# Experts of a mixture: whole low parts on GpSimd, the operand's split on ScalarE and VectorE, and matmuls with the high part ahead of the wait for the low part

## The chip, the core and the metric

The kernel runs on one core of one Trainium2 chip. The core has engines that run side by side and are ordered by semaphores alone: TensorE (matmuls, PE in the profile, with its weight loads as PEld), VectorE (DVE), ScalarE (ACT), GpSimd (POOL) and SyncE (SP), which here only issues DMAs. TensorE, VectorE, ScalarE and GpSimd read and write SBUF; matmul results go to PSUM, eight banks of 512 floats in each of 128 partitions. The metric is the time of the whole program on the device in microseconds, lower being better.

## What is computed

The reference is a two-layer backbone over 512 latent and 256 context tokens of width 1024, in float32. Each layer mixes tokens (four mixers, gates, a projection) and then runs an expert-choice mixture of 16 experts, which is the part that the change touches:

```python
def _expert_choice_ffn(h, w_router, w1, w3, w2):
    cap = CAPACITY_FACTOR * T // N_EXPERTS
    aff = jax.nn.softmax((h @ w_router).astype(jnp.float32), axis=-1)
    vals, idx = lax.top_k(aff.transpose(0, 2, 1), cap)
    xg = jax.vmap(lambda hb, ib: hb[ib])(h, idx)
    hid = jax.nn.silu(jnp.einsum('becd,edf->becf', xg, w1)) * jnp.einsum('becd,edf->becf', xg, w3)
    y = jnp.einsum('becf,efd->becd', hid, w2) * vals[..., None].astype(h.dtype)
    return jax.vmap(lambda yb, ib: jnp.zeros((T, D), h.dtype).at[ib.reshape(-1)].add(yb.reshape(-1, D)))(y, idx)
```

An expert takes 64 latent rows and, in the first layer only, 32 context rows. In the second layer the context is not carried on.

## The kernel before

Matmuls run on operands rounded to a shorter float format. To keep float32 accuracy each operand is split in two: a high part, which is the rounded value (a copy), and a low part, which is the value less the high part (a subtraction). Every product is then three matmuls: high with high, high with low, low with high.

The weights of an expert are three matrices of 1024 x 1024. They are cut in 12 blocks of 512 rows by 512 columns (128 partitions x 2048 floats, 1 MB): blocks 0, 1, 4, 5 of the gate matrix, 2, 3, 6, 7 of the up matrix, 8 to 11 of the down matrix (`expert_block`). Each block b goes through the same stations:

- SyncE issues its DMA into `raw`, a ring of four buffers (`RING`), once the split of the block four places earlier is done (line 594 and the two waits ahead of it).
- ScalarE writes the high part (`hi`, line 1522) into one of three pairs of buffers (`expert_part`, of which two lie in `part` and one in `hx`), once TensorE is done with the block three places earlier (`ring_used`). It counts `split_h`.
- VectorE writes the low part (`rest`, line 2077) and counts `split_v`. For the blocks 1, 3, 5, 7 (`G_HALVES`) it writes half of it, and GpSimd the other half (line 798), counting `split_g`.
- TensorE waits for the low part, all of it, and runs 12 matmuls of 512 columns (line 1253): for each of four slices k the three products.

The expert's rows, `xg_hi` and `xg_lo`, are the other operand of blocks 0 to 7. GpSimd copies and subtracts them (lines 781 and 785), once block 7 of the expert before is done, and TensorE waits for both (`xg`) ahead of an expert.

Each engine works through its own list in order; two experts, an even one (j = 0) and an odd one (j = 1), make one turn of a loop, eight turns a layer. ScalarE and VectorE split two blocks ahead (`AHEAD`): at place b they split block b + 2. Between the splits stand the other steps of an expert. On ScalarE: the Silu behind blocks 1 and 5, the high part of the hidden values (`hd_hi`, at 6 and 9), the high part of y (`y_hi`, line 1546, at 10 and 11, after `val`), and one table load at the start of a turn. On VectorE: the product into `hid` (at 3 and 7), the low part of the hidden values (at 6 and 9), `val` (line 2104, at 9), the matrix `put` that scatters the rows (line 2110, at 10), the low part of y (line 2125, at 10 and 11), and the adds of the scatter results (`add`, line 2085). On TensorE: behind block b of an even expert scatter b - 1 into bank 4, for which it waits for the add of the scatter before (`e_acc`); an odd expert has fewer of them and in the second layer none; the first scatter also waits for the low part of y (`e_yL`). Behind blocks 5 and 8 it transposes the hidden values, which wait for `hid`. On GpSimd: two DMAs (four in the first layer) that fetch `pair` for `val`, which wait until `put` is done (`e_put`), and only behind them the halves of the low parts.

## Time and profile before

| | us |
|---|---|
| median of three runs | 3880.74 (3878.51 to 3883.74) |
| the profiled execution | 3872.74 |
| its span, first to last instruction | 3870.8 |
| TensorE busy in the span | 3418.9 (88%) |
| VectorE busy | 2332.5 (60%) |
| ScalarE busy | 1624.7 (42%) |
| GpSimd busy | 1037.9 (27%) |

The expert stage of the first layer runs from about 1433 to 2130 us of the span, that of the second from about 3205 to 3820. Line 1253, the experts' matmuls, holds 774.6 + 372.7 us of TensorE's busy time. In the profile "busy" is the time from an instruction's start to its end, which includes time in which it is held up while running; a matmul's recorded length (0.39 us) overlaps the next one's, so what counts is the distance between starts. The number in square brackets behind an instruction is how long its engine stood idle before it, and what ended that.

### The profile page before, as it was taken

The page shows a single profiled execution, that of the slowest core. Times are in us where ns is not written, and L with a number is a line of the kernel's source. Part 1 is how long each engine was busy: PE and PEld are TensorE (multiplying, and loading weights), DVE is VectorE, ACT ScalarE, POOL GpSimd, SP SyncE. Part 2 cuts the span into 40 slices and gives each one's busy share as a digit, 9 for nine tenths or more (in the row PEclk, how much of TensorE's full clock was granted, in tenths as well). Part 3 has the DMA queues.
Part 4 walks back from the last instruction along what each step waited for, and adds up shares of the span by engine and source line. Part 5 has one row for each costly group of instructions (what it writes and reads, how often), then busy time and mean ns, then how long its engine had stood idle before and what let it go on. Part 6 is the DMA issues. An engine that isn't in the chain of part 4 may idle for free.

```text
span 3870.8 us, 49033 instructions
## 1 busy us (share of the span) xinstructions
PE 3418.9 (88%) x19072; PEld 2794.2 (72%) x19072; DVE 2332.5 (60%) x3395; ACT 1624.7 (42%) x2095; POOL 1037.9 (27%) x640
## 2 busy tenths in 40 slices
PE   6988899899999969998988199898999969999995
PEld 4988569888887847776776189678866657777774
DVE  2685751511111649989998765751422258999998
ACT  3213752511110236666665322653311126667763
POOL 2001012222120025555554100012222103434442
PEclk8989999999999979999999599998999979999998
DMA  7232034022222329888888122131132217999995
GB/s 241 98 131 94 24 97 143 12 71 67 75 87 77 120 92 313 309 300 307 311 312 318 49 83 78 49 99 55 39 98 98 81 73 265 335 328 342 338 334 205
DMA packets 331926, 633.91 MB, mean 164 GB/s; under 512 B 14526, under 2 KB 104910, under 8 KB 325358
## 3 DMA queue, kind: packets, MB, share of 16 engines
q1 hardware_dynamic: 309056, 557.88, 41.4%
q0 software_dynamic: 22704, 73.73, 5.8%
q8 instruction: 115, 1.88, 0.2%
q14 instruction: 51, 0.42, 0.0%
HBM read 615.05 MB, written 16.50 MB: 163 GB/s over the span
## 4 chain that ended last, share of the span: by engine, by line
PE 64%; DVE 16%; issue 8%; ACT 6%; DMA 3%; POOL 2%; POOLq 1%; DVEq 0%; ACTq 0%; SPq 0%
PE ps L852 42%; PE ps L1253 11%; DVE part L2077 3%; PE ps L977 2%; PE ps L1009 2%; POOL part L798 2%; DVE hx L2077 1%; PE ps L995 1%; ACT hx L1522 1%; DVE area L2085 1%; ACT area L1374 1%; DVE area L1681 1%; PE ps L997 1%; ACT part L1522 1%; DVE area L2104 1%
## 5 line engine op out<-in xcount | busy, mean ns | idle before, releaser
L852 PE MATMUL ps<-hx,part 128*128 128x384 f32 (+2 forms) x4704 | 935.2, 358 | 26.1 <-DVEq L532 22.0
L852 PEld LDWEIGHTS ps<-hx,part 128*128 128x128 f32 x4704 | 835.6, 190 | 114.7 <-DVEq L532 23.6
L1253 PE MATMUL ps<-part,hx 128*128 128x512 f32 x3072 | 774.6, 404 | 104.6 <-POOL part L798 70.9
L1253 PEld LDWEIGHTS ps<-part,hx 128*128 128x128 f32 x3072 | 582.1, 193 | 254.7 <-POOL part L798 85.2
L2077 DVE TENSOR_TENSOR part<-raw,part 128x2048 fp32r<-128x2048 f32 (+1 forms) x256 | 598.6, 2341 | 106.0 <-ACT part L1522 103.5
L1522 ACT ACTIVATE part<-raw 128x2048 fp32r<-128x2048 f32 x256 | 490.2, 1916 | 141.5 <-PE ps L1253 122.9
L518 POOL TENSOR_TENSOR part<-raw,part 128x2048 fp32r<-128x2048 f32 x52 | 238.2, 4580 | 858.7 <-ACT part L515 831.3
L1253 PE MATMUL ps<-hx 128*128 128x512 f32 x1536 | 372.7, 391 | 4.2 <-DVE hx L2077 3.8
L2077 DVE TENSOR_TENSOR hx<-raw,hx 128x2048 fp32r<-128x2048 f32 (+1 forms) x128 | 311.8, 2436 | 49.2 <-ACT hx L1522 48.8
L1253 PEld LDWEIGHTS ps<-hx 128*128 128x128 f32 x1536 | 287.4, 188 | 72.8 <-DVE hx L2077 5.5
L852 PE MATMUL ps<-part,hx 128*128 128x256 f32 (+2 forms) x2208 | 317.1, 306 | 17.7 <-DVEq L532 15.5
L852 PEld LDWEIGHTS ps<-part,hx 128*128 128x128 f32 x2208 | 296.7, 198 | 35.1 <-DVEq L532 16.1
L798 POOL TENSOR_TENSOR part<-raw,part 128x1024 fp32r<-128x1024 f32 x96 | 286.3, 2982 | 128.8 <-ACT part L1522 128.1
L1968 DVE TENSOR_TENSOR area<-ps,area 128x768 f32<-128x768 f32 (+1 forms) x48 | 39.6, 825 | 429.1 <-PE ps L852 429.1
L852 PE MATMUL ps<-area,raw 128*128 128x384 f32 (+1 forms) x768 | 285.3, 521 | 0.0
L1522 ACT ACTIVATE hx<-raw 128x2048 fp32r<-128x2048 f32 x128 | 244.7, 1912 | 25.9 <-PE ps L1253 20.1
L852 PEld LDWEIGHTS ps<-area,raw 128*128 128x128 f32 x768 | 145.0, 190 | 107.9 <-issue 46.0
L1681 DVE SCALAR_TENSOR_TENSOR area<-area,conv_c 128x512 f32<-128x512 f32 x360 | 208.5, 656 | 0.0
L515 ACT ACTIVATE part<-raw 128x2048 fp32r<-128x2048 f32 x76 | 144.8, 1906 | 127.5 <-DMA raw<-in_w_in 93.5
L1473 ACT ACTIVATE area<-ps,mgate_b 128x768 f32<-128x768 f32 x32 | 28.8, 901 | 349.8 <-PE ps L852 349.8
L852 PE MATMUL ps<-raw,area 128*128 128x256 f32 x640 | 144.3, 388 | 10.0 <-DMA raw<-in_w_out 10.0
L852 PEld LDWEIGHTS ps<-raw,area 128*128 128x128 f32 x640 | 124.1, 195 | 28.7 <-issue 11.4
(260 smaller groups left out, 3923.0 us busy)
## 6 DMA issues: line engine op xcount, KB each, us to landing
raw<-in_w_exp_gate SPq DMA_DIRECT2D x128, 1024.0 KB, 5.1
raw<-in_w_exp_up SPq DMA_DIRECT2D x128, 1024.0 KB, 5.4
raw<-in_w_exp_down SPq DMA_DIRECT2D x128, 1024.0 KB, 5.1
raw<-in_w_mod SPq DMA_DIRECT2D x48, 1024.0 KB, 7.7
raw<-in_w_in SPq DMA_DIRECT2D x44, 1024.0 KB, 5.2
raw<-in_w_gate SPq DMA_DIRECT2D x32, 1024.0 KB, 7.9
area<-in_bias POOLq DMA_DIRECT2D x32, 512.0 KB, 4.0
raw<-in_w_branch SPq DMA_DIRECT2D x16, 1024.0 KB, 7.2
```

What stands on the lines that cost most here:

```text
L515: nc.scalar.activation(part[:, q % 2, 0, :], raw[:, n % RING, :], ACT.Copy).then_inc(S("split_h"), 1)
L518: self.tt.tensor_tensor(part[:, q % 2, 1, :], raw[:, n % RING, :], part[:, q % 2, 0, :].bitcast(f32), ALU.subtract).then_inc(S("split_p"), 1)
L798: nc.gpsimd.tensor_tensor(expert_part(s, 1)[:, 2:4, :], raw[:, (r0 + s) % RING, :].rearrange("p (k n) -> p k n", k=4)[:, 2:4, :], expert_p ...
L852: last = mm(dst, a, b, start=i == 0, stop=i == len(pairs) - 1)
L977: last = mm(ps[h2 * HD:(h2 + 1) * HD, 6 + u % 2, 0:P], v, probT[:, w % NTURN, (2 * (b - b0) + h2) * P:(2 * (b - b0) + h2 + 1) * P], start= ...
L995: mm(ps[:, h2, 0:hi - lo], q, k[:, lo:hi], start=True, stop=True)
L1009: last = nc.tensor.transpose(ps[:, 4 + g % 2, o:o + P], prob[:, u % NPROB * 2 + h2, b * P:(b + 1) * P], ident)
L1253: last = mm(ps[:, bank, :], x, y, start=kh == 0 and a == 0, stop=kh == 1 and a == len(pairs) - 1)
L1522: fn(expert_part(s, 0), src, ACT.Copy).then_inc(S("split_h"), 1)
L1681: own(V.scalar_tensor_tensor(y, x, conv_c[:, j, tap:tap + 1], y, ALU.mult, ALU.add))
L1968: V.tensor_tensor(even(t_) if ctx_out else t_[:, 0:LAT], p_, s_, ALU.mult).then_inc(*S("z_part", l).by(1))
L2077: V.tensor_tensor(expert_part(s, 1)[:, ks, :], src[:, ks, :], expert_part(s, 0)[:, ks, :].bitcast(f32), ALU.subtract).then_inc(S("split_v" ...
```

## The change

What it does, by engine:

- The low parts of blocks 2 and 7 are written whole by GpSimd (`G_SPLITS`), those of the other ten whole by VectorE. `rest_rank` says whose a block is and how many of that engine's come before.
- The expert's rows are split by ScalarE (`operand_hi`, at place 8) and VectorE (`operand_lo`, at place 9, ahead of `val`), no longer by GpSimd. GpSimd's list of an expert is then the DMAs of `pair` behind `e_put` and two subtractions.
- TensorE waits at the start of a block for the high part only (`split_h`), runs the eight products with it (`x_hi` and `x_lo`), then waits for the low part and runs the four with that.
- SyncE's DMAs of the experts stand in a loop over eight turns, with computed addresses, instead of 192 instructions a layer. Each waits for one semaphore, that of the engine that wrote the low part four blocks earlier.

```diff
-G_HALVES = (1, 3, 5, 7)
+G_SPLITS = (2, 7)
-NG, NV = len(G_HALVES), EXP_BLOCKS
+NG, NV = len(G_SPLITS), EXP_BLOCKS - len(G_SPLITS)
...
+def rest_rank(s):
     e, b = s // EXP_BLOCKS, s % EXP_BLOCKS
-    return NG * e + sum(g < b for g in G_HALVES)
+    before = sum(g < b for g in G_SPLITS)
+    return (True, NG * e + before) if b in G_SPLITS else (False, NV * e + b - before)
...
+        def operand(e, j, full):
+            src = (xgT[:, :, e, :] if isinstance(e, int) else
+                   xgT[:, :, bass.ds(e, 1), :].rearrange("p k a c -> p k (a c)"))
+            return [(rows_of[j][0], src[:, :, 0:CAPL]), (high_of[j], src[:, :, CAPL:CAP]),
+                            (low_of[j], src[:, :, CAPL:CAP])][:3 if full == NT else 1]
...
-                for s in range(EXP_BLOCKS * E):
-                    name, c, kh = expert_block(s % EXP_BLOCKS)
-                    sp.wait_ge(S("split_v"), v0 + s + 1)
-                    if s >= RING and (s - RING) % EXP_BLOCKS in G_HALVES:
-                        sp.wait_ge(S("split_g"), g0 + halves_before(s - RING) + 1)
+                with sp.Fori(0, E // 2) as i:
+                    for j in range(2 * EXP_BLOCKS):
+                        gps, before = rest_rank(j - RING)
+                        if gps:
+                            sp.wait_ge(S("split_g"), i * 2 * NG + (g0 + before + 1))
+                        else:
+                            sp.wait_ge(S("split_v"), i * 2 * NV + (v0 + RING + before + 1))
+                        src = A[name][l, bass.ds(i * 2 + j // EXP_BLOCKS, 1), kh * NCH:(kh + 1) * NCH, c:c + NCH]
...
-                        pool.wait_ge(ring_used, i * 2 * EXP_BLOCKS + (B_EXP[l] + EXP_BLOCKS * j - 4))
-                        for at, x in moves:
-                            last = nc.gpsimd.tensor_copy(xg_hi[:, :, at], x)
-                        pool.drain()
-                        for at, x in moves:
-                            last = nc.gpsimd.tensor_tensor(xg_lo[:, :, at], x, xg_hi[:, :, at].bitcast(f32), ALU.subtract)
                         pool.wait_ge(*S("e_put", l).at(i * 2 + j + 1))
...
-                        for s in (EXP_BLOCKS * j + b for b in G_HALVES):
+                        for s in (EXP_BLOCKS * j + b for b in G_SPLITS):
                             pool.wait_ge(S("split_h"), i * 2 * EXP_BLOCKS + (h0 + s + 1))
-                            nc.gpsimd.tensor_tensor(expert_part(s, 1)[:, 2:4, :],
+                            nc.gpsimd.tensor_tensor(expert_part(s, 1),
...
-                        pe.wait_ge(*S("xg", l).at(i * 4 + 2 * j + 2))
+                        pe.wait_ge(*S("xg_lo", l).at(i * 2 + j + 1))
-                            pe.wait_ge(S("split_v"), i * 2 * NV + (v0 + RING + s + 1))
-                            if b in G_HALVES:
-                                pe.wait_ge(S("split_g"), i * 2 * NG + (g0 + halves_before(s) + 1))
+                            pe.wait_ge(S("split_h"), i * 2 * EXP_BLOCKS + (h0 + s + 1))
-                            pairs = [(x[:, 4 * kh + k, :], w[u][:, k, :]) for k in range(4)
-                                     for x, u in ((x_hi, 0), (x_hi, 1), (x_lo, 0))]
+                            pairs = [(x[:, 4 * kh + k, :], w[0][:, k, :]) for k in range(4) for x in (x_hi, x_lo)]
+                            pairs += [(x_hi[:, 4 * kh + k, :], w[1][:, k, :]) for k in range(4)]
                             for a, (x, y) in enumerate(pairs):
+                                if a == 8:
+                                    gps, before = rest_rank(s)
+                                    if gps:
+                                        pe.wait_ge(S("split_g"), i * 2 * NG + (g0 + before + 1))
+                                    else:
+                                        pe.wait_ge(S("split_v"), i * 2 * NV + (v0 + RING + before + 1))
...
                         if s + AHEAD < body or not final:
                             hi(i, s + AHEAD)
+                        if b == 8 and not (final and j):
+                            act.wait_ge(ring_used, i * body + (r0 + s))
+                            operand_hi(i * 2 + j + 1, 1 - j)
...
-                        if s + AHEAD < body or not final:
+                        if (s + AHEAD < body or not final) and not rest_rank(s + AHEAD)[0]:
                             rest(i, s + AHEAD)
                         for c in scatters(j, b, per):
                             add(c, 4, i * per)
+                        if b == 9 and not (final and j):
+                            operand_lo(i * 2 + j + 1, 1 - j, i * 2 + j + 2)
```

The diff's pieces are, in this order, of the constants, the helper for the operand, SyncE, GpSimd (twice), TensorE, ScalarE and VectorE.

Three places show what stands where in the engines' lists. Names in square brackets are the semaphores that an instruction waits for. TensorE, blocks 1 and 2 of an even expert, before:

```order
L1253 MATMUL ps<-part,hx 128x512 [waits split_g]
L1253 MATMUL ps<-part,hx 128x512 x11
L1258 ISA [waits e_yL]
L852 MATMUL ps<-hx 128x512 [waits e_acc]
L852 MATMUL ps<-hx 128x512
L1240 REGISTER_ALU
L1253 MATMUL ps<-hx 128x512 [waits split_v]
L1253 MATMUL ps<-hx 128x512 x11
```

And the same blocks in the changed kernel, whose matmuls stand in line 1258:

```order
L1258 MATMUL ps<-part,hx 128x512 [waits split_v]
L1258 MATMUL ps<-part,hx 128x512 x3
L1261 ISA
L1263 ISA [waits e_yL]
L852 MATMUL ps<-hx 128x512 [waits e_acc]
L852 MATMUL ps<-hx 128x512
L1241 REGISTER_ALU
L1258 MATMUL ps<-hx 128x512 [waits split_h]
L1258 MATMUL ps<-hx 128x512 x7
L1255 ISA
L1258 MATMUL ps<-hx 128x512 [waits split_g]
L1258 MATMUL ps<-hx 128x512 x3
```

The wait for the low part moved behind eight of the twelve matmuls, and that for GpSimd from block 1 to block 2.

GpSimd, one expert of the first layer from its last `pair` DMAs on, before:

```order
L789 ISA
L789 DMA area<-slot_d 64x512
L792 ISA
L792 DMA area<-slot_d 64x256
L797 REGISTER_ALU
L798 TENSOR_TENSOR part<-raw,part 128x1024 [waits split_h]
L797 REGISTER_ALU
L798 TENSOR_TENSOR part<-raw,part 128x1024 [waits split_h]
L797 REGISTER_ALU
L798 TENSOR_TENSOR hx<-raw,hx 128x1024 [waits split_h]
L797 REGISTER_ALU
L798 TENSOR_TENSOR part<-raw,part 128x1024 [waits split_h]
```

And now:

```order
L790 ISA
L790 DMA area<-slot_d 64x512
L793 ISA
L793 DMA area<-slot_d 64x256
L798 ISA
L799 TENSOR_TENSOR hx<-raw,hx 128x2048 [waits split_h]
L798 REGISTER_ALU
L799 TENSOR_TENSOR part<-raw,part 128x2048 [waits split_h]
```

Four half subtractions became two whole ones, behind the same DMAs.

VectorE at the end of an even expert of the first layer, from place 9 to the first split of the next expert's block 1, before:

```order
L2077 TENSOR_TENSOR hx<-raw,hx 128x2048 [waits split_h]
L2102 ISA
L2104 SCALAR_TENSOR_TENSOR area<-area,iotas 64x512 [waits pair_in]
L2104 SCALAR_TENSOR_TENSOR area<-area,slot_c 64x256
L2074 REGISTER_ALU
L2077 TENSOR_TENSOR part<-raw,part 128x2048 [waits split_h]
L2110 TENSOR_SCALAR hx<-area,iotas 64x512 [waits e_comb]
L2110 TENSOR_SCALAR hx<-area,slot_c 64x256
L2125 SCALAR_TENSOR_TENSOR hx<-ps,area,hx 64x512 [waits e_yH]
L2125 SCALAR_TENSOR_TENSOR hx<-ps,area,hx 32x512
L2074 REGISTER_ALU
L2077 TENSOR_TENSOR part<-raw,part 128x1024 [waits split_h]
```

And now (rest is in line 2091, `val` in 2127):

```order
L2091 TENSOR_TENSOR hx<-raw,hx 128x2048 [waits split_h]
L2096 ISA
L2098 ISA [waits xg_hi]
L2098 TENSOR_TENSOR hx<-area,hx 128x8x64
L2098 ISA
L2098 TENSOR_TENSOR hx<-area,hx 128x8x32 x2
L2125 ISA
L2127 SCALAR_TENSOR_TENSOR area<-area,iotas 64x512 [waits pair_in]
L2127 SCALAR_TENSOR_TENSOR area<-area,slot_c 64x256
L2089 REGISTER_ALU
L2091 TENSOR_TENSOR part<-raw,part 128x2048 [waits split_h]
```

The operand's subtraction came in ahead of `val`; further down, which is not shown, the low part of block 1 is whole.

## Rows read from the trace of the kernel before

**Rows 1.** Busy time by stretch: us, engines (x count), clock, DMA share, GB/s.

```profile
sum 672.00, PE 605.10 PEld 479.62 DVE 623.77 ACT 443.24 POOL 368.08; mean PE 37.82 PEld 29.98 DVE 38.99 ACT 27.70 POOL 23.01
...
3508.00:3546.50 38.50, 36.72 (x164) 29.58 (x163) 36.48 (x28) 27.43 (x20) 16.12 (x8) 1.00 0.96 345
...
sum 616.00, PE 581.03 PEld 463.32 DVE 564.51 ACT 430.67 POOL 264.78; mean PE 36.31 PEld 28.96 DVE 35.28 ACT 26.92 POOL 16.55
```

**Rows 2.** Waits (us in total, times, longest), layer 0, then layer 1.

```profile
PE ps L1253 <- POOL part L798: 46.3, 15, 3.2
...
PE ps L1253 <- DVE part L2077: 13.9, 18, 1.0
...
PE ps L1253 <- POOL part L798: 19.9, 14, 1.8
```

**Rows 3.** Timeline (start, us, instruction, idle before) of TensorE, layer 0.

```profile
1694.68 3.03 PE L1253 MATMUL ps<-part,hx 128*128 128x512 f32 x12 [0.87 <-DVE part L2077]
1700.87 4.56 PE L1253 MATMUL ps<-part,hx 128*128 128x512 f32 x12 [3.16 <-POOL part L798]
...
1705.78 2.89 PE L1253 MATMUL ps<-hx 128*128 128x512 f32 x12
...
1708.95 2.88 PE L1253 MATMUL ps<-part,hx 128*128 128x512 f32 x12
...
1744.16 3.02 PE L1253 MATMUL ps<-part,hx 128*128 128x512 f32 x12 [3.05 <-POOL part L798]
...
1785.41 3.01 PE L1253 MATMUL ps<-part,hx 128*128 128x512 f32 x12 [3.13 <-POOL part L798]
```

**Rows 4.** Timeline of VectorE, ScalarE and GpSimd at the same boundaries.

```profile
1692.35 2.28 DVE L2077 TENSOR_TENSOR part<-raw,part 128x2048 fp32r<-128x2048 f32 x1
...
1697.09 1.23 DVE L2077 TENSOR_TENSOR part<-raw,part 128x1024 fp32r<-128x1024 f32 x1
...
1702.90 3.39 DVE L2077 TENSOR_TENSOR part<-raw,part 128x1024 fp32r<-128x1024 f32 x1
1706.32 0.69 DVE L2085 TENSOR_TENSOR area<-area,ps 128x512 f32<-128x512 f32 x1
...
1740.37 1.23 DVE L2077 TENSOR_TENSOR part<-raw,part 128x1024 fp32r<-128x1024 f32 x1
...
1698.55 1.90 ACT L1522 ACTIVATE hx<-raw 128x2048 fp32r<-128x2048 f32 x1
...
1696.16 0.52 POOL L789 DMA_DIRECT2D area<-slot_d  x1 [4.03 <-DVE hx L2110]
...
1698.45 2.37 POOL L798 TENSOR_TENSOR part<-raw,part 128x1024 fp32r<-128x1024 f32 x1
1702.33 2.88 POOL L798 TENSOR_TENSOR part<-raw,part 128x1024 fp32r<-128x1024 f32 x1 [1.51 <-ACT part L1522]
```

**Rows 5.** The page's costliest groups: count, busy, mean ns, idle before.

```profile
L2077 DVE TENSOR_TENSOR part<-raw,part 128x2048 fp32r<-128x2048 f32 (+1 forms) x256 | 598.6, 2341 | 106.0 <-ACT part L1522 103.5
...
L518 POOL TENSOR_TENSOR part<-raw,part 128x2048 fp32r<-128x2048 f32 x52 | 238.2, 4580 | 858.7 <-ACT part L515 831.3
...
L2077 DVE TENSOR_TENSOR hx<-raw,hx 128x2048 fp32r<-128x2048 f32 (+1 forms) x128 | 311.8, 2436 | 49.2 <-ACT hx L1522 48.8
```

**Rows 6.** Timeline of a boundary in layer 1: TensorE, VectorE, ScalarE, SyncE's queue.

```profile
3523.56 3.02 PE L1253 MATMUL ps<-part,hx 128*128 128x512 f32 x12 [1.76 <-POOL part L798]
...
3530.35 2.93 PE L1253 MATMUL ps<-part,hx 128*128 128x512 f32 x12
...
3525.58 3.41 DVE L2077 TENSOR_TENSOR part<-raw,part 128x1024 fp32r<-128x1024 f32 x1
...
3521.26 1.90 ACT L1522 ACTIVATE hx<-raw 128x2048 fp32r<-128x2048 f32 x1
...
3525.69 0.37 SPq L594 DMA_DIRECT2D raw<-in_w_exp_up  x1
```

**Rows 7.** Timeline of TensorE, the first expert of layer 0.

```profile
1440.09 5.48 PE L1253 MATMUL ps<-part,hx 128*128 128x512 f32 x12 [8.50 <-POOL hx L785]
```

41 lines of the change are left out of this document (23 added, 18 removed).

## The prediction

> **What bounds the kernel now.** The change touches only the two expert stages, so I went first to the busy time by stretch over each of them [rows 1]. In both, TensorE (37.8 of 42.0 us in layer 0, 36.3 of 38.5 in layer 1) and VectorE (39.0 and 35.3, with the time in which a running instruction is held) are close to full. An expert takes 42.3 us in layer 0 (1700.87 to 1785.41 in rows 3 is a pair, 84.5 us) and 38.0 in layer 1 (pairs of 76.0 us, read from the same block of every second expert). Its work on TensorE is 12 blocks of 2.72 us (rows 3: 1705.78 to 1708.95 is one block and a scatter of 0.45), the scatters and two groups of transposes of 0.35: 37.0 us for an even expert, 34.3 (layer 0) and 33.4 (layer 1) for an odd one. So some 6.6 us of an expert of layer 0 and 2.8 of layer 1 are stall or slow clock.
>
> The list of waits says where they lie [rows 2]: TensorE waits for GpSimd's half low part (46.3 us in layer 0, 19.9 in layer 1) and for VectorE's (13.9). The timeline of a boundary between experts [rows 3] shows it once for all: 0.87 us before block 0, then 3.16 before block 1, whose low half GpSimd starts only at 1698.45, behind the four DMA issues from 1696.16 on that wait for `e_put` [rows 4]. Behind that stall block 1 itself takes 4.56 us where the next expert's takes 3.02: the granted clock had fallen. Over nine boundaries in a row the stall before block 1 is 3.01 to 3.18, and block 1 takes 3.01 to 5.49, on average 1.1 us over 3.02.
>
> The second thing to see is that VectorE and GpSimd exclude each other when both subtract. VectorE's half of block 3 at 1702.90 takes 3.39 us [rows 4] where the undisturbed one at 1697.09 takes 1.23: it ends 1.23 after GpSimd's end at 1705.21, less 0.15. Operations that read PSUM (the add at 1706.32, 0.69) are not held.
>
> **The change part by part.** Times below are on the clock of the boundary in rows 3 and 4, layer 0, into an even expert.
>
> *GpSimd's operand copies move away.* They cost GpSimd some 9 us an expert in layer 0 and hold VectorE at times. On ScalarE a copy of 512 columns is about 0.6 us (it has 2048 in 1.90 [rows 4]), some 1.3 with the two context pieces. It stands at block 8, where ScalarE waits for TensorE anyway: nothing. VectorE's subtraction (same sizes; 2048 in 2.28 at 1692.35) is 0.6 us in layer 1, 1.2 in layer 0, and stands ahead of `val`, for which ScalarE's `y_hi` waits: everything behind it at the boundary comes later. In layer 0 `val` is no longer held by GpSimd's subtraction of the operand, which gives part of it back: the delay is between 0 and 1.2, and I take 0.4 at this boundary, 0.6 at the next; in layer 1 it is the whole 0.6.
>
> *Block 0 and 1.* The low part of block 0 ends at 1692.35 + 0.4 + 2.3 = 1695.0, and TensorE, which can start the first eight products at 1693.81, needs it 1.81 later (8 x 0.227), at 1695.6: the 0.87 goes. Block 1's low part is now whole and VectorE's: 1697.09 + 0.4 to 1699.7. TensorE needs it at 1698.3 and stalls 1.4, ending block 1 at 1700.65; before it was 1705.43. Behind it VectorE still owes the low part of y, 1.5 us, for which the first scatter waits: 1701.65 after it.
>
> *Block 2.* ScalarE's high part ends at 1700.45 + 0.4. GpSimd's whole subtraction is 4.6 (the same operation of the mixers, 52 times, 4.58 on average [rows 5]): 1700.95 to 1705.55. TensorE has the high products by 1703.5 and stalls 2.1; block 2 ends at 1706.45 (before: 1708.50).
>
> *What is queued behind it.* VectorE's next instruction is the low part of block 3. It is held by GpSimd until 1705.55 and ends at 1707.75; behind it stands the add of scatter 0 (to 1708.35), and scatter 1 shares its PSUM bank and waits for this add. TensorE so starts block 3 at 1708.85, against 1708.95 before. **The stall has moved, not gone**, and what is gained is about the 1.5 us of slow clock. From here the walk runs beside the old one: GpSimd's second subtraction runs from about 1716.9 to 1721.5 and TensorE needs it only at 1723.7, VectorE makes the low part of block 8 behind it, until 1723.75, and the transposes behind block 8 fall on 1728.6, against 1728.5 before. So such an expert gains 0: 1.5 of clock regained, 1.4 lost. With the average 1.1 of clock instead, it loses 0.4.
>
> *The odd expert of layer 0* has no table load ahead of ScalarE's high part of block 2 and half the scatters. The same walk from the row at 1740.37 (whole instead of half: to 1743.2) stalls 1.35 at block 1 and 1.0 at block 2, where before it was 0.78 and 3.05, starts block 3 at 1748.8 for 1749.97, loses 0.8 again at block 7 and some 1.7 at the transposes, for which VectorE is late, and comes out 0.85 early without any clock effect, 2.0 with the average of it. A pair gains 1.6, eight pairs **13 us**.
>
> *Layer 1.* Before, the stall ahead of block 1 is 1.76 [rows 6], with the clock at 1.00 [rows 1]. The walk from there: block 1 needs nothing (low part 3522.85), block 2's high part is there at 3523.8 (ScalarE's end at 3523.2, and 0.6) and its low part at 3528.4, VectorE's block 3, before 3525.58 to 3528.99, is held to 3530.6, the add ends at 3531.2, and block 3 starts at 3531.7 where it started at 3530.35. The 1.3 us lost are mostly absorbed by a wait for the down projection's operand at blocks 9 and 10; some 1.0 a pair stays: **8 us lost**.
>
> *First experts.* TensorE's 8.50 us wait for GpSimd's operand [rows 7] ends about 4.3 earlier (a copy of 1.3 and a subtraction of 1.2 instead of GpSimd's 7), but block 2 and its followers give most of it back; walked the same way 1.5 us remain in layer 0, 1.8 in layer 1: **3 us**.
>
> *Waits inside a block* cost nothing if satisfied: 14 starts across a block, a scatter and their waits lie 0.2267 apart on average [rows 3]. SyncE's DMAs move into a loop with computed addresses; the trace has none of SyncE's in that form. GpSimd's, which have it, take 0.52 each [rows 4] where SyncE's take 0.37 [rows 6]. I take nothing, the low bound; 0.15 more on each transfer is hidden while it lands before its buffer's turn, and if layer 1 were bound by them (a DMA share of 0.96 [rows 1]) it would cost 12 x 0.15 x 16 = 29 us. A gain is excluded, since an issue starts on the same event. GpSimd's long hold on one of four ring buffers delays its successor's transfer (issued 3528.4 instead of 3525.69 [rows 6]); it then arrives about when ScalarE may use it (the page gives some 5 us from issue to landing), and VectorE comes to it later still.
>
> The sum: -13 + 8 - 3 = -8 us. The profiled execution took 3872.7 (span 3870.8 and 1.9 around it), so 3864.7 on its scale; the median of the three runs is 8.0 above the profiled one, and on that scale the forecast is 3880.7 - 8 = **3873 us**.
>
> **The rivals.** *The stalls really go.* If GpSimd and VectorE overlap better than rows 4 suggest, TensorE saves its waits for low parts, 46.3 + 13.9 + 19.9 = 80 us, and 18 of clock (1.1 x 16): 3880.7 - 98 = 3783. For it speaks that low parts are now needed 1.8 us later in every block; against it that block 2 waits for a 4.6 us operation that can't start before ScalarE's high part. Half of it would be 3832.
>
> *The lock makes VectorE the bound (slower).* Per expert VectorE's undisturbed subtractions go from 8 x 2.29 + 4 x 1.23 = 23.2 to 22.9 + 1.2 us, and GpSimd's hold is 9.2. VectorE's two groups of subtractions [rows 5] come to 910 us in 32 experts, 28.4 each, so before 5.2 of GpSimd's time fell on VectorE; my walk puts 4.1 there. If all 9.2 does, VectorE is busy 39.2 (39.0 of 42.0, scaled to 42.3) + 0.9 + 4.0 = 44.1 of 42.3: 1.8 more x 16 = 29, and in layer 1, 34.8 + 0.3 + 4.0 against 38.0, 1.1 x 16 = 18: 3880.7 + 47 = 3928. It decides from 7.4 of the 9.2 in layer 0. The Trainium skill (Perfetto Trace Analysis, Optimizing Scalar/DVE Operations) speaks against such a move in general: offloading between these two "might not help", as they share a port. By that rule this rival is the likeliest; the trace agrees that they exclude each other (the row at 1702.90), but not that it decides, since VectorE stood only 5.2 of some 14 us of GpSimd's work.
>
> *The clock stays low as often.* The walk leaves 6 us of idle in 10 around blocks 1 to 3 of even experts, in pieces up to 2.1. If the clock falls there as it does now, 18 us of regained clock go: 3891.
>
> **How the numbers follow.** The moved stall 0.50 (3860 to 3890), stalls gone in good part 0.23, clock low 0.12, VectorE the bound 0.15. The likeliest gives 3873; the range 3815 to 3910 reaches half way into both outer cases and covers half of the price of slower issues. About 0.2% (7.8 us) is what a measurement of this kernel can tell from no change. Of the moved stall I put half beyond it on the fast side (0.25), 0.18 inside, 0.07 slower; so faster 0.25 + 0.23 = 0.48, same 0.20, slower 0.07 + 0.12 + 0.15 minus 0.02 that end within = 0.32.
>
> **What would show it.** In the changed profile: no wait for GpSimd ahead of block 1; instead one of 1 to 2 us inside block 2 behind GpSimd's 4.6 us; VectorE's subtraction of block 3 held to some 5 us; scatter 1 waiting for the add; layer 0 near 41.4 us an expert, layer 1 near 38.5. Wrong, if block 3's subtraction is not held, if transfers take visibly longer to issue, or if layer 1 gets shorter.

## The result, and the profile after

| | median us | range of the runs | profiled execution | its span | mean granted clock |
|---|---|---|---|---|---|
| before | 3877.55 | 3873.19 to 3883.74 (7 runs) | 3872.74 | 3870.8 | 0.943 |
| after | 3893.88 | 3889.69 to 3905.27 (7 runs) | 3893.88 | 3892.2 | 0.945 |

The changed kernel is slower: the ratio is 1.0054, with a 95% interval of 1.0042 to 1.0067. The medians are 16.3 us apart and the profiled executions 21.1. The forecast was 3873, some 8 us faster. The sign was wrong.

The first question is in which stage the loss lies. Both kernels have the same short transposes of the routing (line 1196) ahead of each layer's expert stage, and the stage ends with the last scatters. In the kernel before they lie here (timeline of TensorE; start, us, instruction, idle before and what ended it):

```profile
1384.96 0.82 PE L1196 MATMUL ps<-consts,area 16*128 16x16 f32 x6 [15.99 <-DVE area L2048]
...
2122.13 5.37 PE L852 MATMUL ps<-hx 128*128 128x512 f32 x16 [3.02 <-DVE hx L2125]
...
3166.93 0.60 PE L1196 MATMUL ps<-consts,area 16*128 16x16 f32 x4 [16.16 <-DVE area L2048]
...
3827.60 4.02 PE L852 MATMUL ps<-hx 128*128 128x512 f32 x16 [1.56 <-DVE hx L2125]
```

and the changed kernel here:

```profile
1381.98 0.82 PE L1196 MATMUL ps<-consts,area 16*128 16x16 f32 x6 [16.01 <-DVE area L2063]
...
2122.14 5.51 PE L852 MATMUL ps<-hx 128*128 128x512 f32 x16 [4.63 <-DVE hx L2148]
...
3167.54 0.60 PE L1196 MATMUL ps<-consts,area 16*128 16x16 f32 x4 [16.16 <-DVE area L2063]
...
3848.08 5.54 PE L852 MATMUL ps<-hx 128*128 128x512 f32 x16 [1.81 <-DVE hx L2148]
```

Layer 0 ends at the same time to 0.01 us, but that is chance: its stage began 3.0 us sooner, behind code that the change does not touch. In the 14 profiled executions of this case that first row lies anywhere within 8.3 us, so only the distance within a stage can be compared. By that the stage of layer 0 took 740.2 us for 737.2, 3.0 more, and that of layer 1 680.5 for 660.7, 19.9 more. Nearly all of the loss is in layer 1, and nothing of the forecast 13 us was won in layer 0.

The boundary that the prediction walked through, into an even expert of layer 0, stands in the changed kernel's timelines of TensorE, VectorE and GpSimd as follows; [rows 3] and [rows 4] are the same places before.

```profile
1699.26 1.20 PE L1258 MATMUL ps<-part,hx 128*128 128x512 f32 x4 [1.49 <-DVE part L2091]
...
1705.05 1.19 PE L1258 MATMUL ps<-hx 128*128 128x512 f32 x4 [1.59 <-POOL hx L799]
1707.92 0.72 PE L852 MATMUL ps<-hx 128*128 128x512 f32 x2 [1.67 <-DVE area L2106]
1708.48 2.92 PE L1258 MATMUL ps<-part,hx 128*128 128x512 f32 x12
...
1702.17 4.98 DVE L2091 TENSOR_TENSOR part<-raw,part 128x2048 fp32r<-128x2048 f32 x1 [1.42 <-ACT part L1527]
1707.18 0.69 DVE L2106 TENSOR_TENSOR area<-area,ps 128x512 f32<-128x512 f32 x1
...
1700.42 4.58 POOL L799 TENSOR_TENSOR hx<-raw,hx 128x2048 fp32r<-128x2048 f32 x1 [2.18 <-ACT hx L1527]
```

Read it down. TensorE waits 1.49 us inside block 1 for VectorE's whole low part, and 1.59 inside block 2 for GpSimd's (4.58 us). VectorE's low part of block 3 starts 1.75 after GpSimd's, takes 4.98 instead of 2.28, and ends 2.15 after GpSimd does. The add stands behind it, and the second scatter waits 1.67 for the add. So one wait of 3.16, with one of 0.87 ahead of it, became three of 1.5 to 1.7.

The same boundary in layer 1, where before there was one wait of 1.76 [rows 6] and a granted clock of 1.00 in every window but the stage's first:

```profile
3618.86 1.19 PE L1258 MATMUL ps<-hx 128*128 128x512 f32 x4 [1.79 <-POOL hx L799]
3621.73 1.22 PE L852 MATMUL ps<-hx 128*128 128x512 f32 x2 [1.68 <-DVE area L2106]
3622.75 5.12 PE L1258 MATMUL ps<-part,hx 128*128 128x512 f32 x12
```

A scatter of two matmuls takes 1.22 where it takes 0.62 at full clock, and block 3 takes 5.12 for 2.88: 2.8 us more. Short windows of the changed kernel over this place (us, busy time of PE, PEld, DVE, ACT and POOL, granted clock, DMA share, GB/s) show it as clock:

```profile
3609.80:3616.20 6.40, 6.40 (x30) 5.30 (x29) 4.50 (x5) 6.32 (x7) 3.01 (x3) 1.00 0.97 329
3616.20:3622.60 6.40, 2.94 (x10) 1.82 (x9) 6.37 (x3) 3.76 (x3) 2.61 (x1) 0.85 0.88 283
3622.60:3629.00 6.40, 6.40 (x19) 5.01 (x19) 4.71 (x5) 1.54 (x2) 0.00 (x0) 0.62 1.05 392
```

In the middle window TensorE was busy 2.94 of 6.40 us. In the next its mean clock is 0.62, so for most of it the lower of the two levels, 1.2 GHz, was granted.

TensorE's waits by what ended them (us in total, times, longest), layer 0 and then layer 1, against [rows 2]:

```profile
PE ps L1258 <- DVE part L2091: 21.9, 16, 1.5
PE ps L1258 <- POOL hx L799: 14.2, 14, 1.6
PE ps L852 <- DVE area L2106: 12.6, 8, 1.7
PE ps L1231 <- DVE area L2140: 11.1, 8, 1.4
...
PE ps L1258 <- POOL hx L799: 15.3, 15, 1.8
PE ps L852 <- DVE area L2106: 11.7, 7, 1.7
```

The 46.3 and 19.9 us for GpSimd are down to 14.2 and 15.3, but waits that hardly existed now stand beside them: for the add (none in layer 0 before), and for the product that the transposes read (the line L1231; 1.1 us in layer 0 before).

The costliest groups of the page (count, busy, mean ns, idle before) answer to [rows 5]:

```profile
L2091 DVE TENSOR_TENSOR part<-raw,part 128x2048 fp32r<-128x2048 f32 x224 | 602.3, 2692 | 39.1 <-ACT part L1527 37.8
...
L2091 DVE TENSOR_TENSOR hx<-raw,hx 128x2048 fp32r<-128x2048 f32 x96 | 243.7, 2538 | 58.5 <-ACT hx L1527 58.3
```

VectorE's subtractions of weights went from 910 to 846 us, and its whole busy time, with the operand's subtraction added, from 2332.5 to 2294.6. VectorE got freer and the kernel slower: its total was not the point, but when it is held.

An expert's length is best read from one group of transposes behind block 8 to the next. There are 15 such periods a layer, by turns odd and even:

| us | layer 0 odd | layer 0 even | layer 1 odd | layer 1 even |
|---|---|---|---|---|
| before, sum of 8 odd / 7 even | 330.0 | 304.7 | 290.4 | 280.6 |
| after | 322.4 | 314.7 | 294.2 | 296.5 |
| before, each | 40.9 to 42.1 | 43.5 to 43.9 (one 42.3) | 36.2 to 36.6 | 39.7 to 40.4 |
| after, without a fall of the clock | 40.1 to 41.0 | 43.8 (one 42.5) | 36.4 to 37.3 | 40.9 to 41.2 |
| after, with one | 40.3 (1 of 8) | 46.6 to 47.5 (3 of 7) | – | 42.6 to 44.0 (4 of 7) |

### The profile page after: what moved, and what is told of

The parts are those of the page before. It is cut to its first block, busy times and chain, and to the rows that moved or that the text cites. A ratio compares the mean times of both kernels' runs of the same rounds, so it can differ in the third digit from the quotient of the medians.

```text
span 3892.2 us, 49875 instructions
## 1 busy us (share of the span) xinstructions
PE 3418.3 (88%) x19072; PEld 2791.6 (72%) x19072; DVE 2294.6 (59%) x3395; ACT 1646.9 (42%) x2159; POOL 748.9 (19%) x448
## 3 DMA queue, kind: packets, MB, share of 16 engines
q1 hardware_dynamic: 309056, 557.88, 41.6%
## 4 chain that ended last, share of the span: by engine, by line
PE 62%; DVE 12%; ACT 10%; issue 9%; DMA 5%; POOLq 1%; POOL 1%; DVEq 1%; ACTq 0%; SPq 0%
PE ps L852 42%; PE ps L1258 9%; ACT hx L1527 3%; DVE part L2091 2%; ACT part L1527 2%; PE ps L977 2%; PE ps L1009 2%; DMA raw<-in_w_exp_up 2%; DMA raw<-in_w_exp_down 2%; PE ps L995 1%; ACT area L1379 1%; DVE area L1696 1%; ACT area L1307 1%; PE ps L997 1%; POOLq L542 1%
## 5 line engine op out<-in xcount | busy, mean ns | idle before, releaser
L1258 PE MATMUL ps<-part,hx 128*128 128x512 f32 x3072 | 763.7, 401 | 39.2 <-DVE part L2091 21.9
L2091 DVE TENSOR_TENSOR part<-raw,part 128x2048 fp32r<-128x2048 f32 x224 | 602.3, 2692 | 39.1 <-ACT part L1527 37.8
L1258 PE MATMUL ps<-hx 128*128 128x512 f32 x1536 | 381.7, 394 | 37.4 <-POOL hx L799 36.9
L528 POOL TENSOR_TENSOR part<-raw,part 128x2048 fp32r<-128x2048 f32 x52 | 238.2, 4581 | 857.4 <-ACT part L525 830.0
L2091 DVE TENSOR_TENSOR hx<-raw,hx 128x2048 fp32r<-128x2048 f32 x96 | 243.7, 2538 | 58.5 <-ACT hx L1527 58.3
L799 POOL TENSOR_TENSOR part<-raw,part 128x2048 fp32r<-128x2048 f32 x32 | 148.5, 4641 | 377.0 <-ACT part L1527 377.0
L799 POOL TENSOR_TENSOR hx<-raw,hx 128x2048 fp32r<-128x2048 f32 x32 | 149.4, 4668 | 40.7 <-ACT hx L1527 40.7
```

Of the source, the lines that this page charges most:

```text
L528: self.tt.tensor_tensor(part[:, q % 2, 1, :], raw[:, n % RING, :], part[:, q % 2, 0, :].bitcast(f32), ALU.subtract).then_inc(S("split_p"), 1)
L799: nc.gpsimd.tensor_tensor(expert_part(s, 1), raw[:, (r0 + s) % RING, :].rearrange("p (k n) -> p k n", k=4), expert_part(s, 0).bitcast(f32) ...
L1258: last = mm(ps[:, bank, :], x, y, start=kh == 0 and a == 0, stop=kh == 1 and a == len(pairs) - 1)
L2091: V.tensor_tensor(expert_part(s, 1), src, expert_part(s, 0).bitcast(f32), ALU.subtract).then_inc(S("split_v"), 1)
```

## The experiments

Each was timed against the kernel before. Ratios are to that, with their 95% intervals. A difference between two of the kernels is given by their medians and by their ratios, since these come out some us apart.

**Is the new loss clock, or the waits themselves?** The first run fills the waits with 11 matmuls in every even expert, whose results nothing uses. The second takes away one wait, that of the second scatter for the add.

```diff
+                                if a == 8 and b == 2 and j == 0:
+                                    for d in range(6):
+                                        mm(ps[:, 7, :], x_hi[:, d, :], x_hi[:, 0:4, :], start=True, stop=True)
                                 if a == 8:
...
+                            for d in range(5 if b == 2 and j == 0 else 0):
+                                mm(ps[:, 7, :], x_hi[:, d, :], x_hi[:, 0:4, :], start=True, stop=True)
                             for c in scatters(j, b, per):
```

> The changed kernel, with eleven extra matmuls per even expert whose results nobody reads: six of 512 columns in block 2 ahead of the wait for GpSimd's low part (1.4 us of a stall of 1.6) and five behind block 2 ahead of the scatter that waits for the add (1.1 of 1.7). They do no work of the kernel; they only keep TensorE busy. Theory A (the moved stall itself costs about nothing on average, and the loss comes from the clock, which now falls behind these stalls in both layers): even experts of 43.8 us in layer 0 and 41.2 in layer 1 without exceptions, granted clock 1.00 throughout both stages, about 17 us faster than the changed kernel, 3874 to 3880. Theory B (VectorE or the transfers are the bound, the clock only follows): no change or a few us slower than the changed kernel, 3894 to 3902, even where the clock is 1.00.

Measured: 3878.53 us (3871.84 to 3883.96), ratio 1.0006 (0.9997 to 1.0015), 15 us less than the changed kernel by the medians and 19 by the ratios, as theory A had it. The same boundary in its timeline of TensorE (L1254 and L1266 are the added matmuls):

```profile
1698.40 1.52 PE L1254 MATMUL ps<-hx 128*128 128x512 f32 x6
1700.17 1.20 PE L1261 MATMUL ps<-hx 128*128 128x512 f32 x4 [0.25 <-POOL hx L799]
1701.21 1.31 PE L1266 MATMUL ps<-hx 128*128 128x512 f32 x5
1703.05 0.73 PE L852 MATMUL ps<-hx 128*128 128x512 f32 x2 [0.53 <-DVE area L2111]
1703.61 2.90 PE L1261 MATMUL ps<-part,hx 128*128 128x512 f32 x12
```

TensorE still waits for GpSimd and for the add, 0.25 and 0.53 behind its filling, and block 3 takes 2.90. The long periods are gone: even experts of layer 1 take 41.2 to 41.6 (one 40.3), those of layer 0 43.5 to 44.0. Useless work made the kernel faster, so these 15 to 19 us were clock: between the first and the last transposes of layer 1 the granted clock is 1.00, where the changed kernel has 0.98. In the profiled execution the even experts took 16.0 us less over both layers. The odd ones, in which nothing was filled, took 6.3 more, for which no run shows the reason. The 1.1 us by which an even expert of layer 1 exceeds the one before is still there; it is the waits' own.

```diff
+                        early = b == 1
+                        for c in scatters(j, b, per) if early else ():
+                            add(c, 4, i * per)
                         if (s + AHEAD < body or not final) and not rest_rank(s + AHEAD)[0]:
                             rest(i, s + AHEAD)
-                        for c in scatters(j, b, per):
+                        for c in scatters(j, b, per) if not early else ():
                             add(c, 4, i * per)
```

> The changed kernel, but at place 1 VectorE does the add of the scatter result ahead of block 3's low part, which GpSimd holds up. Theory A (what stands queued behind the held subtraction is what TensorE waits for): the 1.7 us wait of scatter 1 goes in every even expert of both layers, some 1.5 x 16 = 24 us, and with it part of the clock's falls, another 5 to 15: 3855 to 3868. Theory B (VectorE is full, so its work only changes its order): 3888 to 3900, the 1.7 us turning up as a wait for the low part in block 3 or for hid.

Measured: 3865.30 us (3857.60 to 3871.65), ratio 0.9970 (0.9959 to 0.9980). Moving one addition of 0.69 us ahead of the held subtraction turns the changed kernel from slower than before to faster, 29 us by the medians and 33 by the ratios, which is theory A. In its timelines of VectorE and TensorE in layer 1:

```profile
3586.92 0.69 DVE L2106 TENSOR_TENSOR area<-area,ps 128x512 f32<-128x512 f32 x1 [1.24 <-PE ps L852]
3587.53 4.93 DVE L2091 TENSOR_TENSOR part<-raw,part 128x2048 fp32r<-128x2048 f32 x1
...
3590.36 1.20 PE L1258 MATMUL ps<-hx 128*128 128x512 f32 x4 [1.66 <-POOL hx L799]
3591.40 0.62 PE L852 MATMUL ps<-hx 128*128 128x512 f32 x2
```

VectorE is held as long as before, 4.93, but the scatter starts without a wait. The wait for GpSimd stays, and alone it did not bring the clock down here.

**One part of the change alone: the order of the products.** In the kernel before, TensorE's wait for the low part goes behind the eight products with the high part; nothing else changes.

```diff
-                            pe.wait_ge(S("split_v"), i * 2 * NV + (v0 + RING + s + 1))
-                            if b in G_HALVES:
-                                pe.wait_ge(S("split_g"), i * 2 * NG + (g0 + halves_before(s) + 1))
+                            pe.wait_ge(S("split_h"), i * 2 * EXP_BLOCKS + (h0 + s + 1))
...
+                                if a == 8:
+                                    pe.wait_ge(S("split_v"), i * 2 * NV + (v0 + RING + s + 1))
+                                    if b in G_HALVES:
+                                        pe.wait_ge(S("split_g"), i * 2 * NG + (g0 + halves_before(s) + 1))
```

> The kernel before with one part of the change alone: TensorE waits for the high part, runs the eight products with it, then waits for the low part; GpSimd still makes halves for blocks 1, 3, 5, 7 and the operand. Theory A: block 1 of an expert ends 0.9 us behind GpSimd's half instead of 2.7, which shortens the loop from one boundary to the next by up to 1.8 us in both layers, 1.8 x 32 = 58, plus the clock no longer falling in layer 0, 10 to 18: 3800 to 3830. Theory B (VectorE gives it back later in the expert): 3855 to 3875.

Measured: 3877.88 us (3867.43 to 3889.56), ratio 1.0002 (0.9990 to 1.0014): nothing in the sum, and my theory A was wrong. In the profiled execution the 15 periods of layer 0 are 5.7 us shorter than before and those of layer 1 13.7 us longer, at a granted clock of 0.98 for 1.00. The timeline of TensorE at the place of [rows 6], with the two rows of VectorE behind it, shows why:

```profile
3524.40 2.91 PE L1256 MATMUL ps<-hx 128*128 128x512 f32 x12
3529.11 0.73 PE L852 MATMUL ps<-hx 128*128 128x512 f32 x2 [1.81 <-DVE area L2088]
3529.68 4.50 PE L1256 MATMUL ps<-part,hx 128*128 128x512 f32 x12
...
3524.90 3.43 DVE L2080 TENSOR_TENSOR part<-raw,part 128x1024 fp32r<-128x1024 f32 x1
3528.37 0.69 DVE L2088 TENSOR_TENSOR area<-area,ps 128x512 f32<-128x512 f32 x1
```

The wait of 1.76 ahead of block 1 is gone, and TensorE runs into the add instead, 1.81, and then has a slow block. The kernel before has the same trap: its low part of block 3 is held too (3.41 at 3525.58 in [rows 6]), but TensorE came late enough not to notice.

**Is that the whole reason?** The same kernel with the addition first, and the addition first without the new order.

```diff
+                        early = b == 1
+                        for c in scatters(j, b, per) if early else ():
+                            add(c, 4, i * per)
                         if s + AHEAD < body or not final:
                             rest(i, s + AHEAD)
-                        for c in scatters(j, b, per):
+                        for c in scatters(j, b, per) if not early else ():
                             add(c, 4, i * per)
```

> The kernel before with two edits of TensorE's and VectorE's order: the products with the high part first, and at place 1 of every expert VectorE's addition of scatter 0 ahead of its low part of block 3. Theory C (the wait has moved): in the run with the products' order alone, TensorE no longer waits 1.76 us ahead of block 1 but 1.81 us ahead of scatter 1, for an addition that stands behind VectorE's held subtraction (21 us in both layers' boundaries), and the clock falls behind it in layer 1. With the addition first both go: some 21 us of waits and some 10 of clock, 3840 to 3855, even experts of layer 1 near 38. Rival D (VectorE's time is the bound, and which of its instructions comes first decides nothing): the subtraction of block 3 comes later and TensorE waits for it instead, 3868 to 3880.

> The kernel before with only the addition of scatter 0 ahead of VectorE's low part of block 3. Theory C: in the kernel before TensorE waits 0.3 us in all for an addition, since the long stall ahead of block 1 gives VectorE the time for it; the edit is worth nothing there, within 4 us of the kernel before. Rival D': the addition first is worth 20 us by itself, whatever the products' order, 3850 to 3860.

Measured: both edits 3850.79 us (3848.91 to 3860.97), ratio 0.9952 (0.9939 to 0.9965). The addition alone, 3868.64 (3861.85 to 3875.97), ratio 0.9986 (0.9973 to 0.9999), 5 us by the ratio where within 4 was forecast. So by the ratios the order of the products is worth nothing alone, the addition 5 us, and both together 19 (by the medians 2 lost, 7 and 25 won), which is theory C; only its even experts of layer 1 are not near 38 but 39.1 to 40.5. Two waits stood one behind the other: hiding the first showed the second, and taking away the second alone won little while the first stood.

**The order of the products inside the change.** The wait goes back to the head of the block; the products keep their order.

```diff
-                                if a == 8:
+                                if a == 0:
                                     gps, before = rest_rank(s)
```

> The changed kernel with the wait for the low part back at the head of each block; the order of the products stays. Theory F (inside the change the order ahead of the wait is what hides the 1.8 us of each late low part): each of the 45 waits counted inside blocks gets up to 1.8 us longer, half of it caught up later, and the clock falls oftener: 3925 to 3965. Rival G (as in the kernel before, where the same edit alone was worth nothing in the sum): 3890 to 3905.

Measured: 3894.41 us (3889.07 to 3897.97), ratio 1.0055 (1.0036 to 1.0074), as the changed kernel, and as rival G had it. Theory F was wrong. At the boundary of layer 0, timeline of TensorE:

```profile
1699.78 3.01 PE L1258 MATMUL ps<-part,hx 128*128 128x512 f32 x12 [1.70 <-DVE part L2091]
...
1705.56 4.50 PE L1258 MATMUL ps<-hx 128*128 128x512 f32 x12 [2.31 <-POOL hx L799]
1709.90 0.63 PE L852 MATMUL ps<-hx 128*128 128x512 f32 x2
```

The waits ahead of the blocks are longer, but the second scatter no longer waits for its add. Earlier products only bring TensorE sooner to the same late row of VectorE.

**The place of GpSimd's operation.** The changed kernel with the addition first, and with GpSimd's first whole low part at block 4.

```diff
-G_SPLITS = (2, 7)
+G_SPLITS = (4, 7)
```

> The changed kernel with the addition first, and with GpSimd's two whole low parts at blocks 4 and 7 instead of 2 and 7. Theory E (the place of GpSimd's operation decides): the wait inside block 2 for GpSimd (7.5 us in layer 0 and 14.7 in layer 1 of the run with the addition first) goes, VectorE is no longer held at block 3 but behind it, where less waits: 3840 to 3855. Rival D (the lock takes the same time of VectorE wherever it stands): the wait comes back as one for VectorE's low part in block 2 or 5, 3862 to 3872.

Measured: 3898.02 us (3895.00 to 3906.26), ratio 1.0070 (1.0050 to 1.0089): 33 to 39 us worse than with block 2. Neither theory had that sign. TensorE's waits for VectorE's low parts in layer 0 (us in total, times, longest), and two rows at an odd expert of that layer (timelines of GpSimd and VectorE):

```profile
PE ps L1258 <- DVE part L2091: 56.6, 24, 4.0
...
1744.06 4.58 POOL L799 TENSOR_TENSOR part<-raw,part 128x2048 fp32r<-128x2048 f32 x1 [5.18 <-ACT part L1527]
...
1744.35 6.43 DVE L2091 TENSOR_TENSOR part<-raw,part 128x2048 fp32r<-128x2048 f32 x1
```

The wait inside block 2 is gone, as theory E had it, but the waits for VectorE grew from 21.3 us to 56.6. The rows show where: GpSimd's low part of block 4 starts 0.29 us ahead of VectorE's of block 3, which so takes 6.43, and TensorE, which needs block 3 first, waits 4.01 for it. This is so in the odd experts of layer 0 alone, whose eight periods grew from 324.5 to 354.0. In layer 1 block 4 was no worse: its 15 periods took 579.8 us for 582.0, the odd ones 283.7 for 299.6. So block 2 was the better place in layer 0 only; block 2 in one layer and block 4 in the other was not tried.

**The other part alone: the operand.** The kernel before, with the operand's copies on ScalarE and its subtraction on VectorE, as in the change; then, in the changed kernel with the addition first, the operand back on GpSimd; and, in that kernel again, VectorE's subtraction behind `val`.

> The kernel before with another part alone: ScalarE and VectorE split the operand, nothing else. Theory A: VectorE's subtraction of 0.6 us (1.35 in layer 0, less what val no longer waits) stands on the chain from block 8 to GpSimd's first half, so an expert gets 0.5 to 0.7 us longer, 16 to 22 us in all, less some 4 us at the first expert: 3890 to 3898. Theory B (GpSimd's copies were what held VectorE): 5 to 15 us faster than before, 3862 to 3872.

> The changed kernel with the addition first, and with the operand's copies and subtraction back on GpSimd, ahead of its DMA issues; the two whole low parts stay. Theory H (the operand's subtraction of 1.36 us in layer 0 and 0.69 in layer 1 is paid in full, since VectorE's chain is what ends last at the boundary): the 15 us that moving it alone had cost come back, 3846 to 3856. Rival K (the cost of the move is absorbed beside the whole low parts, and GpSimd's 9 us of operand hold VectorE as much): 3860 to 3870.

```diff
-                        if b == 9 and not (final and j):
-                            operand_lo(i * 2 + j + 1, 1 - j, i * 2 + j + 2)
                         sets = ((0, LAT, rows_of[j][0]), (LAT, TOK, rows_of[j][1]))[:2 if ctx_out else 1]
...
                             last.then_inc(*S("e_val", l).by(1))
+                        if b == 9 and not (final and j):
+                            operand_lo(i * 2 + j + 1, 1 - j, i * 2 + j + 2)
```

> The changed kernel with the addition first, and with VectorE's subtraction of the operand behind val instead of ahead of it, so that ScalarE's high part of y, which waits 43.9 us for val in layer 0, has it 1.4 us sooner. Theory L (val is what the subtraction delays): 3852 to 3860. Theory H (VectorE's chain as a whole: the low parts of blocks 0 and 1 come as late in either order): 3862 to 3868.

Measured: the operand alone 3890.57 us (3886.97 to 3901.11), ratio 1.0039 (1.0026 to 1.0051), as expected. The operand back, 3857.56 (3847.77 to 3860.55), ratio 0.9947 (0.9932 to 0.9961): 8 or 9 us of the 15, between the two theories. Behind `val`, 3853.78 (3851.95 to 3855.16), ratio 0.9946 (0.9933 to 0.9960): 9 to 11.5 us less than with the addition first alone (3865.30), theory L. The run with the operand alone has VectorE at the boundary so (timeline, layer 0):

```profile
1692.12 1.36 DVE L2090 TENSOR_TENSOR hx<-area,hx 128x512 fp32r<-128x512 f32 x3
```

The three subtractions, 1.36 us together, stand ahead of `val`, which starts at 1693.51, and ScalarE's high part of y waits for `val`. ScalarE's wait for it in layer 0 is, with the subtraction first:

```profile
ACT hx L1560 <- DVE area L2130: 43.9, 16, 3.7
```

and behind `val`:

```profile
ACT hx L1560 <- DVE area L2128: 24.8, 16, 3.7
```

In the changed kernel the move itself was not the price; its place in VectorE's order was. With `val` first the operand off GpSimd is about as good as on it.

**The division of the low parts, alone and in company.** The kernel before with the products' order and the addition first; VectorE makes the low part of block 1 whole, and GpSimd keeps three halves. Then the same with the operand moved, its subtraction behind `val`.

```diff
-G_HALVES = (1, 3, 5, 7)
+G_HALVES = (3, 5, 7)
```

> The kernel before with the products' order, the addition first, and one piece of the change's new division: VectorE makes the low part of block 1 whole, GpSimd keeps the lower halves of blocks 3, 5 and 7 alone. Theory J (block 1 waits for GpSimd because of its four DMA issues, not for want of VectorE's time): in the run with the first two edits TensorE waits 31.6 us in layer 0 for GpSimd's half of block 1, some 2.0 an expert; VectorE's whole one ends about 1.0 later than TensorE's first eight products, so half of it goes, and some clock: 3830 to 3842. Rival D (VectorE's time is the bound): the 1.1 us more on VectorE come back at blocks 2 and 3: 3847 to 3856.

> The kernel before with the products' order, the addition first and VectorE's whole block 1 (the fastest run so far, 3848), and with the operand's copies on ScalarE and its subtraction on VectorE behind val. Theory M (in layer 0 VectorE's time is now the bound: its rows stand end to end, and 1.36 us of subtraction comes to them for about as much of GpSimd's hold, while layer 1 pays 0.69 an expert): 3846 to 3858. Rival N (GpSimd's 9 us of operand work hold VectorE by more than 1.36 in layer 0, as the shorter experts of layer 0, 40.1 and 41.5 us, in the run with val first suggest against 41.1 and 41.8 here): layer 0 gains 10 to 15 us, 3832 to 3842.

Measured: 3848.09 us (3844.66 to 3851.88), ratio 0.9936 (0.9922 to 0.9949), which is the lowest of all runs; and 3853.28 (3847.56 to 3860.31), ratio 0.9951 (0.9938 to 0.9965), theory M. In the first, the wait for GpSimd's half of block 1 is gone, but the gain is 2.7 us against 3850.79 by the medians, 6 by the ratios, whose intervals overlap; the time is rival D's. The 15 periods of layer 0 in the run without and in the run with the whole block 1 show that it is two effects (us, busy time of PE, PEld, DVE, ACT and POOL, granted clock, DMA share, GB/s):

```profile
1466.09:2080.44 614.35, 564.34 (x2425) 449.79 (x2423) 594.17 (x480) 421.75 (x313) 364.42 (x217) 0.98 0.93 316
...
1472.90:2094.70 621.80, 569.94 (x2425) 441.73 (x2423) 612.82 (x480) 421.75 (x313) 367.20 (x202) 0.99 0.93 312
```

In layer 0 VectorE is busy 612.82 of 621.80 us, held time included, and the periods got 7.5 us longer: there rival D holds. In layer 1 they got shorter, 560.9 us for 572.7, as theory J would have it. The whole block 1 in layer 1 alone was not tried. The second run, with the operand moved too, has 621.7 us in layer 0 and 571.3 in layer 1, which in the sums fits theory M. But the 10.4 us more in layer 1 are in the even experts alone, some of them at a lower clock (0.99 for 1.00), not 0.69 in each.

| kernel | us | ratio |
|---|---|---|
| changed kernel | 3893.88 | 1.0054 |
| with unused matmuls in the waits | 3878.53 | 1.0006 |
| with the addition first | 3865.30 | 0.9970 |
| and the operand behind `val` | 3853.78 | 0.9946 |
| and instead the operand on GpSimd | 3857.56 | 0.9947 |
| before, products' order and addition first | 3850.79 | 0.9952 |
| and block 1 whole on VectorE | 3848.09 | 0.9936 |

## Why the prediction was wrong

**What held.** The walk through the boundary was right to 0.6 us in each step: 1.49 for 1.4 in block 1, 1.59 for 2.1 in block 2, VectorE's block 3 to 1707.15 for 1707.75, the scatter behind the add, and block 3 at 1708.48 for 1708.85. An even expert of layer 0 without a fall of the clock takes 43.8 against 43.6 to 43.9 (forecast: 0). An odd one gained 0.95 (7.6 in 8) where the walk without clock had 0.85. In layer 1 the walk's "some 1.0 a pair" came out at 1.1. SyncE's issues with computed addresses still take 0.37 each, in the changed kernel as in [rows 6]; the register instructions ahead of an issue take 0.03 to 0.04 us each, and no run tries them alone:

```profile
3576.39 0.37 SPq L607 DMA_DIRECT2D raw<-in_w_exp_gate  x1
```

**What failed**, on the scale of the profiled executions (-8 forecast, +21.1 measured). The parts below come to +23.5; -0.6 lie behind the last transposes, and the rest outside the two stages, in code that the change does not touch:

1. *The regained clock, layer 0: -13 forecast, +2.4 measured over the 15 periods.* The step is "A pair gains 1.6", which put the average 1.1 us of clock on top of the odd expert's 0.85, as if every microsecond of slow clock lengthened the expert. The odd experts did have such falls, 5 of 8 of them, with a block 1 of 4.48 to 5.49 us. But here are two of them, with a fall and without (timeline of TensorE, kernel before):

```profile
1489.30 4.61 PE L1253 MATMUL ps<-part,hx 128*128 128x512 f32 x12 [3.04 <-POOL part L798]
...
1574.14 3.02 PE L1253 MATMUL ps<-part,hx 128*128 128x512 f32 x12 [3.01 <-POOL part L798]
```

The first has lost 1.6 us more in block 1, and its period is 40.9 us against 41.1 of the second. In the second TensorE waits for VectorE instead, 0.21, 0.28 and 0.38 us up to the transposes, where the first has no wait. Only the two falls of 2.5 us made an odd expert longer, by some 0.9. So 8 x 1.1 = 9 us of gain did not exist. In the even experts a fall did cost 1.3 to 1.6 of the period (43.6 to 43.9, without one 42.3), but the moved stall took the same back, as forecast, and the fall did not always go: in 3 of 7 it moved to block 3, where it cost 2.8 to 3.7 us, 9.4 in all.
2. *The clock in layer 1, which had no term: +8 forecast, +19.7 measured over the 15 periods.* The walk kept the clock at 1.00 behind the moved waits. Its own loss held: without a fall an even expert takes 41.2 for 40.1 on average before, some 8 us in 7, and the run with the unused matmuls shows the same. What it lacked are four falls of the clock, of 1.4 to 2.8 us each, another 8, and 0.5 us in each odd expert, 4.
3. *First experts: -3 forecast, +0.8 in layer 0 and +0.6 in layer 1*, from the row of line 1196 to the transposes behind block 8. Their first waits answer to [rows 7] (timeline of TensorE):

```profile
1432.64 7.37 PE L1258 MATMUL ps<-part,hx 128*128 128x512 f32 x24 [4.02 <-ACT part L1527]
...
1446.53 2.08 PE L1258 MATMUL ps<-hx 128*128 128x512 f32 x4 [4.26 <-POOL hx L799]
...
3220.53 1.41 PE L1258 MATMUL ps<-hx 128*128 128x512 f32 x4 [3.23 <-POOL hx L799]
```

The wait for the operand was forecast well: TensorE starts 7.5 us sooner in layer 0, of which 3.0 lie ahead of the stage and 4.5 are the operand's (forecast 4.3), and 2.2 sooner in layer 1. But it gives back all of that, not most: 4.26 and 3.23 in block 2 for GpSimd's whole low part, 0.80 and 1.34 for the add, and a block 3 of 4.23 and 4.71 us at the lower clock.

**The rivals.** "The clock stays low as often" gave 3891 at a chance of 0.12, and came nearest to the number, in part by luck. It was right that the regained clock would be no gain. But in layer 0 the clock did not fall as often: blocks slowed by it are in 11 of the 15 periods before and in 4 after, and the granted clock rose from 0.97 to 0.98. What cost the time are falls in layer 1, where this rival had none. I had written that 6 us of idle in 10 are left around blocks 1 to 3, in pieces up to 2.1; that row spoke for falls, and most of all in layer 1, where a fall was a new loss. "VectorE is the bound" was wrong for this kernel. It needed 7.4 of GpSimd's 9.2 us an expert to fall on VectorE; the page's 846 us are 26.4 an expert, 3.5 over the undisturbed 22.9, and my walk had 4.1. VectorE is busy 90% of layer 0's periods and 86% of layer 1's. The Trainium skill (SBUF — State Buffer, Who interferes with whom) says that a VectorE instruction with two SBUF inputs contends with a GpSimd instruction that reads SBUF, and that the second to start "fully blocks"; the rows agree (4.98 and 4.93 for 2.28). Here the hold took less of VectorE's time than before (3.5 us an expert for 5.2), and cost much where it fell ahead of the add.

**What stays open.** Why a boundary with the same waits had a fall in 3 or 4 of 7 experts and none in the others isn't settled: the pieces are alike (1.49, 1.59, 1.67 at the boundary shown, without a fall; 1.79 and 1.68 at the one of layer 1, with one). The 0.5 us by which layer 1's odd experts got longer have no run of their own, but they go with GpSimd's whole low part at block 2: the six kernels that have it take 294.2 to 303.4 us for the eight periods, the one with it at block 4 takes 283.7, the kernel before 290.4. ScalarE's waits for the transfers of up weights are longer in layer 1 (24.1 us for 8.9), which fits GpSimd's longer hold on its buffer, but that is only argued. The unrolled loop of SyncE was not tried inside the changed kernel.

## What to carry to other kernels

When a walk shows that a wait moves, look at what is queued behind the operation that now ends it: here an addition of 0.69 us behind a held subtraction of 4.98, and moving the addition was worth some 30 us, more than either part of the change that was timed alone (nothing, and 15 lost). Price the clock by place: a fall counts only where no other engine sets the end of the stretch, a granted clock of 1.00 can only get worse, and one long wait cut into several short ones, with little work between them, can lose it. Compare two profiles from a row just ahead of the stage, not by the time since the start. An edit that hides one wait says little until the next wait behind it is gone too: try both together before dropping either.

## What the runs showed of the chip

- Two waits of 1.79 and 1.68 us with four matmuls between them brought TensorE's clock to its lower level, as one wait of 3.16 did, and the fall then cost 2.8 us behind them (5.12 for 2.88, 1.22 for 0.62) instead of 1.5 (4.56 for 3.02). Three of 1.49, 1.59 and 1.67 did not bring it down. Single waits were not alike: behind 1.76 the clock stayed [rows 6], behind 1.81 it fell (4.50 for 2.91).
- Eleven unused matmuls in each even expert, some 2.5 us (11 x 0.227) of TensorE's time that would have been idle, gave back 15 to 19 us of the kernel.
- A fall of the clock need not cost time: 1.6 us lost in block 1 left three odd experts of layer 0 at 40.9 to 41.0 us, where the three without a fall took 41.0 to 41.1.
- The hold between VectorE and GpSimd goes both ways. With VectorE running first, GpSimd's subtraction took 5.73 instead of 4.58 (at 3629.47 us, in layer 1 of the run with its first low part at block 4).
